# Six changes of place in a two-layer decoder trunk: sums, activations, a quad, banks, first slots, one transfer

## The reference

```
for layer in range(DEPTH):                      # DEPTH = 2
    mixer = fox_mixer if layer % 2 == 0 else retention_mixer
    h = h + mixer(rmsnorm(h, norm[layer]), ...)
    h = h + square(relu(rmsnorm(h, mlp_norm[layer]) @ w_up)) @ w_down
return rmsnorm(h, final_norm)

def rmsnorm(x, g): return x * rsqrt(mean(x * x) + 1e-6) * g
retention: o = scores(q, k, decay) @ v + (q * decay) @ state; o = norm_per_head(o) * gn
           return (silu(h @ wg) * o) @ wo
```

## Time and profile before

| quantity | value |
|---|---|
| median of three runs | 2526.87 us |
| profiled execution, and its span | 2525.21 us, 2523.3 us |
| TensorE busy | 2499.7 us, 99% |
| DVE busy | 1902.9 us, 75% |
| ACT busy | 1413.9 us, 56% |
| bytes moved | 518 MB, 205 GB/s |

### The profile page before, as it was taken

One profiled execution on the slowest core, in us unless ns is written; L12 is line 12 of the kernel. 1 busy time (PEld: TensorE's weight loads), 2 busy tenths in 40 slices (PEclk: granted clock), 3 DMA queues, 4 the chain that ended last, 5 costly groups with the idle time before them and its releaser, 6 DMA issues.

```text
span 2523.3 us, 30224 instructions
## 1 busy us (share of the span) xinstructions
PE 2499.7 (99%) x11250; PEld 2061.9 (82%) x11250; DVE 1902.9 (75%) x2110; ACT 1413.9 (56%) x1705; POOL 114.4 (5%) x192
## 2 busy tenths in 40 slices
PE   9999999999999999999999999999999999999998
PEld 7888887888888888888888888887878888888887
DVE  6455465787887877887777877777988788788786
ACT  7444444554646556655556546555556565565564
POOL 0000000100000000000000000000010000010000
PEclk9999999999999999999999999999999999999999
DMA  8445455565756656665564655556667475656473
GB/s 308 155 151 173 144 193 213 202 226 191 250 192 223 227 205 229 224 212 187 191 199 167 227 190 180 177 186 204 232 218 266 170 255 185 239 205 241 169 271 133
DMA packets 143414, 518.04 MB, mean 205 GB/s; under 512 B 17456, under 2 KB 17712, under 8 KB 142384
## 3 DMA queue, kind: packets, MB, share of 16 engines
q1 hardware_dynamic: 131328, 476.65, 53.8%
q0 software_dynamic: 11808, 39.33, 4.9%
q10 hardware_dynamic: 144, 0.26, 0.0%
HBM read 498.35 MB, written 17.83 MB: 205 GB/s over the span
## 4 chain that ended last, share of the span: by engine, by line
PE 92%; DVE 3%; DMA 2%; ACT 1%; issue 1%; SPq 0%; DVEq 0%; ACTq 0%
PE acc L862 12%; PE acc L864 12%; PE acc L863 12%; PE sc L864 11%; PE sc L863 11%; PE sc L862 11%; PE acc L643 4%; PE acc L645 4%; PE acc L644 4%; DVE w_lo L1867 1%; PE mix L862 1%; PE mix L864 1%; PE mix L863 1%; DMA raw<-in_w_stream 1%; PE tr L661 1%
## 5 line engine op out<-in xcount | busy, mean ns | idle before, releaser
L1867 DVE TENSOR_TENSOR w_lo<-raw,w_hi 128x1024 fp32r<-128x1024 f32 x694 | 846.9, 1231 | 328.0 <-ACT w_hi L1299 325.3
L1299 ACT ACTIVATE w_hi<-raw 128x1024 fp32r<-128x1024 f32 x694 | 731.8, 1059 | 630.1 <-PE sc L864 212.1
L862 PE MATMUL acc<-w_hi,xT_hi 128*128 128x512 f32 x826 | 323.7, 392 | 5.8 <-DVE xT_lo L1932 2.7
L864 PE MATMUL acc<-w_hi,xT_lo 128*128 128x512 f32 x826 | 322.4, 390 | 0.0
L863 PE MATMUL acc<-w_lo,xT_hi 128*128 128x512 f32 x826 | 322.3, 390 | 0.0
L1299 ACT ACTIVATE w_hi<-scratch 128x1024 fp32r<-128x1024 f32 x203 | 213.6, 1059 | 176.4 <-PE sc L864 61.4
L1867 DVE TENSOR_TENSOR w_lo<-scratch,w_hi 128x1024 fp32r<-128x1024 f32 x203 | 246.3, 1221 | 78.9 <-ACT w_hi L1299 78.1
L862 PE MATMUL sc<-w_hi,xT_hi 128*128 128x512 f32 x736 | 287.7, 391 | 0.0
L864 PE MATMUL sc<-w_hi,xT_lo 128*128 128x512 f32 x736 | 286.7, 390 | 0.0
L863 PE MATMUL sc<-w_lo,xT_hi 128*128 128x512 f32 x736 | 286.5, 389 | 0.0
L862 PE MATMUL acc<-w_hi,aT_hi 128*128 128x512 f32 x600 | 235.2, 392 | 4.5 <-issue 4.3
(11 more groups left out here) (266 smaller groups left out, 3907.3 us busy)
## 6 DMA issues: line engine op xcount, KB each, us to landing
raw<-in_w_stream SPq DMA_DIRECT2D x725, 512.0 KB, 4.6
scratch<-in_w_stream SPq DMA_DIRECT2D x170, 512.0 KB, 5.6
park<-stage POOLq DMA_DIRECT2D x30, 512.0 KB, 2.9
evac<-park POOLq DMA_DIRECT2D x120, 128.0 KB, 3.1
gain<-in_gains POOLq DMA_DIRECT2D x4, 1024.0 KB, 6.8
h<-in_x SPq DMA_DIRECT2D x2, 1024.0 KB, 8.7
scratch<-in_gn POOLq DMA_DIRECT2D x8, 256.0 KB, 4.6
scratch<-in_x_t SPq DMA_DIRECT2D x3, 512.0 KB, 8.5
```

The costliest lines, as they stand in the source:

```text
L862: pe.matmul(bank[:, :], x_hi, w_hi[:, c], start=start, stop=False, skip_group_check=True)
L864: return pe.matmul(bank[:, :], x_lo, w_hi[:, c], start=False, stop=stop, skip_group_check=True)
L1299: act.activation(w_hi[:, slot * SW:(slot + 1) * SW], mlp_raw(u, load_of(u, t)), ACT.Copy).then_inc(mlp_hi, 1)
L1867: dve.tensor_tensor(w_lo[:, c], mlp_raw(u, load_of(u, t)), w_hi[:, c].bitcast(F32), ALU.subtract).then_inc(mlp_lo, 1)
```

## The change

There are six things. (1) In every seven_pair TAU3 comes before TAU1: the load order, the high halves, the low halves and the matmuls of the two change places, while DVE makes the two sums in the order of before. (2) In the last output projection pairs' first one of each half, the batches of the last head's quad are called after B22 and TAU4 rather than after tiles 7 and 8; ACT and DVE make their halves one to two tiles earlier. (3) Quad 2 of the retention norm is transposed by PE in the last pair of the first MLP (after tiles 15 and 16) rather than by the turn; the turns behind it are numbered one lower. (4) The last norm weight is fetched after all turns rather than before the turns of the second MLP. (5) The last fox block writes the mix banks, and the first pair waits for one add less at its start. (6) The first two slots of the stream are loaded and split in halves, with the first pieces of x transposed smaller, and the first two matmuls stand ahead of the wait for the low half.

More of the change, by code:

```diff
@@ L216, in list_staged @@
 def list_staged():
+    ups = [OF_FOUR] * SUPER
     staged, of_turn = QUADS, []
[L219 to L222, removed]
+    for turns in (*ups, OF_RET_NORM, None, OF_FOUR, *ups):
+        if turns:
+            of_turn += [staged + q + 1 for q in range(turns)]
+        staged += QUADS if turns else 2 * RET_HEADS
     return of_turn
@@ L626, in _, with product @@
             T = Tally("block", "tr0", "tr1", "staged0", "staged1", "group", "ret_head")
-            def product(lhs, tok, first, last, fresh=False):
+            def product(lhs, tok, first, last, fresh=False, banks=acc):
                 hi_t, lo_t = lhs
@@ L699, in both_of_slot @@
                         bank = banks[tok]
-                        pe.matmul(bank[:, :], xT_hi[:, x_cols], w_hi[:, w_cols], start=(kt == 0), stop=False)
+                        if not first:
+                            pe.matmul(bank[:, :], xT_hi[:, x_cols], w_hi[:, w_cols], start=(kt == 0), stop=False)
                         pe.matmul(bank[:, :], xT_hi[:, x_cols], w_lo[:, w_cols], start=False, stop=False)
@@ L909, in plain_pair @@
                 for t in range(TOKS):
-                    pe.wait_ge(acc_out[t], T("block"))
+                    pe.wait_ge(acc_out[t], T("block", -1))
                 for t in range(2 * SLOTS):
                     half, s = t // SLOTS, t % SLOTS
+                    if t == SLOTS:
+                        for tok in range(TOKS):
+                            pe.wait_ge(acc_out[tok], T("block"))
                     if half == 0 and s == SLOTS - 2:
@@ L1144, in _ @@
             act.activation(evac[0][:, 0:1], stage[0][:, 0:1], ACT.Copy)
-            x_hi(0)
-            act.wait_ge(half_in, 16)
-            act.activation(w_hi[:, 0:NB], raw[:, 0:NB], ACT.Copy).then_inc(half_hi, 1)
-            x_hi(1)
-            act.wait_ge(raw_in[0], 16)
-            act.activation(w_hi[:, NB:SW], raw[:, NB:SW], ACT.Copy).then_inc(hi_made, 1)
-            for s in range(1, SLOTS):
+            for s in range(IN_HALVES):
+                for kk in range(PER_SLOT):
+                    x_hi(2 * s + kk)
+                    c = slot_cols(s, kk)
+                    act.wait_ge((half_in, raw_in)[kk][s], 16)
+                    act.activation(w_hi[:, c], raw[:, c], ACT.Copy).then_inc((half_hi, hi_made)[kk], 1)
+            for s in range(IN_HALVES, SLOTS):
                 x_hi(2 * s)
@@ L1509, in query_key_block @@
                     square_of_h(1, QUADS - 2, z_out, done)
-                    for t in range(1, 6):
+                    for t in range(1, 4):
                         hi(u, t)
+                    batch_hi(0, xT_hi, QUADS - 2)
+                    hi(u, 4)
+                    batch_hi(1, xT_hi, QUADS - 2)
+                    hi(u, 5)
                     square_of_h(0, QUADS - 1, e_out, done)
@@ L1880, in first_pair @@
                     lo(u, t)
-                add(1, n)
+                add(1, n, mix)
                 dve.wait_ge(acc_out[1], T("block", 1))
@@ L2128, in seven_pair @@
                     dve.wait_ge(gain_in, T("norm") * 16)
-                    gained_after(0, quad, x_out, done + 1)
+                    if quad == OF_RET_NORM and scaled:
+                        dve.wait_ge(parked, 16 * MLP_NORM_AT)
+                    gained_after(0, quad, x_out, done + 1, stage if quad == OF_RET_NORM and scaled else tr)
             def mlp_pair(m, i):
@@ L2223, in value_gate_pair @@
                 tau13(u)
+                lo(u, TAU3)
+                if turns:
+                    batch_lo(0, *turned, quad)
                 lo(u, TAU1)
                 tau2(u)
-                if turns:
-                    batch_lo(0, *turned, quad)
-                lo(u, TAU3)
                 if turns:
```

103 lines of the change are left out of this document (52 added, 51 removed).

## The result

The changed kernel takes 2535.36 us, the median of six runs (2531.61 to 2541.85), against 2525.76 for six runs of the kernel before on the same chips. The ratio is 1.0043 with the 95% interval 1.0027 to 1.0059: slower by about 11 us. The profiled execution took 2534.57 with a span of 2532.7, which is 9.4 more than before.

The account below looks back on a forecast made before the run. TensorE, busy 2499.7 of 2523.3 us, was taken to bound the kernel. Terms +7.05 −1.25 +0.8 −0.1 +0 −0.1 +0.4 gave +6.8: 2532.0 us profiled, 2533.7 median; 8-in-10 range 2524.5 to 2538.

Parts of the forecast that it names:

- The largest term: TAU3 before TAU1 in down pairs and units 19 and 29: DVE idles one activation per pair, +7.05 us.
- the quad's term: Retention quad 2 through TensorE's transposes, counted at the last batch's low half near 1117 us: net +0.8 us.
- 1.09 on DVE costs 1.09 on TensorE: Unit 2: the chain from the sum to TensorE has no slack, so DVE's 1.09 us idle reaches TensorE whole.
- The forecast of 6.55 for the down pairs: First down pairs each pay 1.09 us less their slack, unit 10 nothing: 6.55 us together.
- Unit 10: A wait for TensorE breaks the chain there, so the delayed sums do not reach the load: 0.
- Output pairs: Units 24 and 34: new 3.0 us stall ahead of transpositions, bank's and turned operand's waits removed: −0.1 and −1.15, together −1.25.
- rival 1: Every stall goes and nothing takes its place: −13.2 us, 2513.7 us; chance 0.14.
- Clock: One chance in eight of losing 1.6 us at each new output-pair gap, unit 36's loss unchanged: +0.4 us.
- Rival 3: The clock falls in both new output-pair gaps, 3.2 in place of 0.4: +9.6 us, 2536.5 us; chance 0.12.
- Norm weight: Moving the last 1 MB transfer gains 0.8 us in unit 36 and costs 0.7 in unit 50: net −0.1.
- Quad, banks, first slots: Retention quad by TensorE +0.8 us, last fox block's mix banks 0, first slots in halves −0.1.
- rival 2: DVE's idle activation is absorbed, so 7.05 falls away: −0.25 us, 2526.6 us, no change; chance 0.20.

Follow-up runs that it names:

- sums_only: Kernel before with only TAU3 ahead of TAU1: 2534.03 us against 2524.47, ratio 1.0036.
- wo_split: Changed kernel with TensorE's transpositions in units 24 and 34 back behind tiles 7 and 8, ACT's and DVE's halves still early: 2533.98 us, ratio 1.0032.
- late_weight: Changed kernel with the last norm weight's transfer held back until the last pair has begun: 2532.81 us in one run.
- weight_back: Changed kernel with the last norm weight's transfer at its old place, ahead of the second MLP's turns: 2533.51 us in one run.
- no_sums: Changed kernel with TAU1 ahead of TAU3 again, the five other parts kept: 2523.36 us, ratio 0.9991.
- best_plain: Kernel before with ACT's and DVE's batch halves early, TensorE's transpositions in their old place and the norm weight late, sums unchanged: 2518.98 us, ratio 0.9977.
- fill_idle: Changed kernel with DVE's block transposition for the turn moved between the two sums and the first low half: 2525.68 us in one run.
- fill_timed: Same kernel as fill_idle, timed against the kernel before: 2525.05 us against 2525.30, ratio 0.9997.
- the three best kernels: Kernel before with early ACT and DVE batch halves and late norm weight; two also have the swap with DVE's idle time filled: ratios 0.9984, 0.9977, 0.9981.
- best_filled: As best_plain, plus TAU3 ahead of TAU1 with the block transposition in DVE's idle time: 2521.21 us against 2525.30 before, ratio 0.9984.

## Why the prediction was right, and where it was off
The forecast was +6.8 to 2533.7; measured is 1.0043, some +11, in the range. The largest term and its mechanism were right. That the total came so near is in part luck: in unit 36 a loss of 1.7 and a gain of 1.6 that were not forecast cancel, and the swap's cost at the first head stood in the quad's term.

- **Sums.** The step "1.09 on DVE costs 1.09 on TensorE" holds: idle 1.19 in the row, and the loss goes when the idle time is filled. The forecast of 6.55 for the down pairs stands against 7.8 in the trace after (with unit 50's transfer in it) and 9.1 in sums_only. Unit by unit it was poor. Unit 10 was put at 0 and paid 0.96 and 1.19; units 2, 6, 14 and 42 paid less than forecast. The seven pairs other than unit 50 cost 3.5 to 7.6 in the five traces that have the swap with its idle time (after, sums_only, wo_split, late_weight, weight_back), 5.6 by the forecast. Slack read to a tenth from one execution does not hold in the next. That it would be 0 in unit 10 was an inference from one break in a chain, and was wrong. As a price for all edits of the swap the ratios say 9 alone (6 to 12, which holds 7.05) and 13 on top of the other parts. The traces after and no_sums end 9.9 apart: 6.0 at the eight down pairs, 0.5 in units 19 and 29, 1.0 at the first head, 1.5 of clock in unit 24. The last two are the swap's too, and were not in its term.
- **A wait not seen.** In unit 36 TensorE waits 1.50 for DVE's product in stage, ahead of the batch; tile 9 was the only place that I had compared. The traces show where it comes from. Some 20 us earlier ACT waits for a load of unit 35, and from that tile's high half to the product in stage it is always the same: 20.6 us in before, no_sums and best_plain, 20.9 in the kernels with the filled swap, 21.5 in those with the swap and its idle time (21.3 in sums_only). What differs is when the load lands. Its high half starts 20.4 us ahead of TensorE's last matmul before the batch in after, 19.8 in no_sums, 20.1 in late_weight and 20.4 in wo_split, and these four wait; it starts 21.4 ahead in before and 22.0 to 23.0 in weight_back, fill_idle, fill_timed and the three best kernels, and these don't. sums_only lies between, with 21.3 and a wait of 0.4. In after, no_sums and weight_back it is:

```profile
1821.68 1.06 ACT L1329 ACTIVATE w_hi<-raw 128x1024 fp32r<-128x1024 f32 x1 [1.40 <-DMA raw<-in_w_stream]
...
1816.24 1.06 ACT L1329 ACTIVATE w_hi<-raw 128x1024 fp32r<-128x1024 f32 x1 [0.23 <-DMA raw<-in_w_stream]
...
1823.55 1.06 ACT L1329 ACTIVATE w_hi<-raw 128x1024 fp32r<-128x1024 f32 x1 [0.38 <-DMA raw<-in_w_stream]
```

  So some 0.9 of the 1.7 is the swap's idle activation in unit 36 and the rest the load's; why the load was late in some executions is open.
- **Output pairs.** The stall was put at 2.9 to 3.0 and is 2.97. The net without clock was put at −0.1 and −1.15 (its own terms give 0.0 and −1.0): measured −0.1 (no_sums and fill_timed, where the clock held) and −1.1. The bank's wait that went was paid in full at the next place, as rival 1 denied.
- **Clock.** In the trace after, one of the two new stalls cost 1.5 and unit 36's loss of 1.6 went, so +0.4 stands against −0.1. The chance of one in eight for each stall was too small all the same. Of ten such stalls of 2.8 us in the five traces that have them (after, fill_idle, fill_timed, late_weight, weight_back), eight were followed by a fall of the granted clock, at 1.3 to 2.8 us each; the two of 1.6 in no_sums by none. In all twelve traces, past the first 100 us, it fell behind 14 of the 19 stops of TensorE of 2.4 us and more, the shortest 2.46, and behind none of the 33 of 1.25 to 1.85. Length doesn't decide between 2.4 and 2.9: 2.47 was followed by a fall twice (sums_only), 2.88 was not (unit 50 above). By the Trainium skill's "TensorE: Matmul & The Clock Gate", section "HAM oscillation — how this bites in real kernels", stops between bursts bring the slow clock back, and the traces agree in 14 of these 19 cases. Rival 3, put at 0.12, has both stalls cost clock, which three of the five traces show, though not the changed kernel's own; its 2536.5 is as near to the result as the forecast.
- **Norm weight.** The sum was put at −0.1 with an explanation for unit 36 that fell: with the transfer in the same place ACT waited 1.34 and 1.56, so 2.76 was no sign of it. Its size in unit 50, 0.7, was 2.1 to 2.3 in this trace. I had compared the transfer's place with the load's only by nearness. The Trainium skill's rule in "DMA: Bandwidth & Descriptors", section "Issuing engines are not separate DMA queues", that transfers of all engines interleave on the same 16, agrees with unit 50, and not with the 2.76 for which the prediction cited it; the rows add that only a transfer issued shortly ahead of the load delayed it (4.12 at 1.85 us ahead, 1.33 at 3.00 ahead, 1.34 at 1.16 behind).
- **Quad, banks, first slots.** +0.8 was exact, from 0.83 in unit 15 and 0.0 at the first head. It holds only together with the swap: in no_sums the first head gives 1.0 back. Banks and slots are below what the traces tell apart: at the second pair the shift is +0.2, +0.1 and 0.0 in the changed kernel, no_sums and fill_timed, +1.9 in wo_split, whose clock fell in the first 20 us, and +0.3 in sums_only, which has neither.

Rival 1 (everything saved) is out by the stalls; rival 2 (absorbed) by sums_only.

What stays open: why a particular load lands late in an execution (unit 35 in after and no_sums, unit 36 in the profile before and in best_filled), which moves single steps by 1 to 2 us, and what decides whether a stall of 2.4 to 2.9 us costs the clock.

## What to carry to other kernels
When two engines work alternately on a chain, ask what the second waits for after a change of order. Here the order of two tiles cost an engine one idle activation of 1.1 us in each pair, and an independent piece of its own work put into the hole took the loss away. A wait that is removed at one place is worth nothing until the next wait that ends at a fixed time has been looked at; moving ACT's and DVE's halves alone (wo_split, best_plain) removed the wait at tile 11 and made no stall. A transfer that nobody is in a hurry for is issued after the load that the critical chain needs, not merely somewhere else.

## What the runs showed of the hardware
A transfer issued by one engine delayed a load issued by another, but only when it went out shortly ahead. The 1 MB norm weight, issued by POOL 1.85 us ahead of a 512 KB load of SP, left ACT idle for 4.12 us (after) and 3.63 (wo_split); 3.00 ahead it left the wait at 1.33 (no_sums), and 1.16 and 1.17 behind at 1.34 and 1.56 (weight_back, sums_only). In the eight traces in which it stands among these loads, it and they landed in the order of issue.

TensorE's granted clock fell behind 14 of 19 stops of 2.4 us and more and behind none of 33 of 1.25 to 1.85 us. So one long stop can cost more than two short ones of about the same sum: unit 24 steps by −0.1 in no_sums, with stops of 1.0 and 1.5 us, and by +1.45 in the changed kernel, with one of 2.8 and the clock's fall behind it.
